# Mixture layers: the first turn's weight units before TensorE's branch, and buffers freed by ScalarE

## The reference

```python
g_sel = argmax(p_g); w_g = max(p_g)              # top-1 of 4 groups
top_v, top_i = lax.top_k(sel, 2)                 # top-2 of the 8 experts in the group
gate = w_g[:, None] * softmax(top_v)
y = (silu(x @ w_gate[e]) * (x @ w_up[e])) @ w_down[e]   # 32 experts, width 256
out[token] += y * gate
```

## Time and profile before

| | us |
|---|---|
| runs before, median of 3 | 2005.03 (2000.83 to 2006.79) |
| the profiled execution | 2006.36 |
| its span, first to last instruction | 2004.5 |
| TensorE busy | 1783.8 (89%) |
| VectorE busy | 1085.9 (54%) |
| ScalarE busy | 644.9 (32%) |
| first mixture layer, from the router to its last addition | about 34 to 273.7 |
| second mixture layer | about 436 to 676.0 |

### The profile page before, as it was taken

The page is one execution under the profiler, slowest core; times in us unless marked ns, Lnnn a source line. Parts: engine busy times, 40 slices in busy tenths (PEclk is TensorE's granted clock), DMA queues, the critical chain, the costliest instruction groups (busy, mean ns, idle before and its releaser), DMA issues. The chain is left out here.

```text
span 2004.5 us, 29934 instructions
## 1 busy us (share of the span) xinstructions
PE 1783.8 (89%) x12646; PEld 1318.7 (66%) x12646; DVE 1085.9 (54%) x1973; ACT 644.9 (32%) x1013; POOL 10.5 (1%) x6
## 2 busy tenths in 40 slices
PE   6888789888887899989996999999998988769998
PEld 5332266573322588878875788878886877557887
DVE  4332243353322577742378586677666564558665
ACT  3111012241110444422233554455443502136443
POOL 0000000000000000000000000000000000100000
PEclk9898889788988899999997899999999989679999
DMA  9899971358999955513420355535542412044540
GB/s 362 368 420 421 421 280 36 132 196 360 422 420 421 384 181 184 182 59 114 181 84 1 126 210 187 188 129 195 187 167 95 147 41 87 4 147 168 189 168 22
DMA packets 58189, 405.26 MB, mean 202 GB/s; under 512 B 6416, under 2 KB 7824, under 8 KB 10432
## 3 DMA queue, kind: packets, MB, share of 16 engines
q1 hardware_dynamic: 58048, 403.25, 52.4%
HBM read 402.18 MB, written 1.05 MB: 201 GB/s over the span
## 5 line engine op out<-in xcount | busy, mean ns | idle before, releaser
L1995 PE MATMUL ps<-ffn_x,ffn_wh 128*128 128x512 f32 x1408 | 497.1, 407 | 9.9 <-DVE ffn_x L2129 7.1
L1998 PE MATMUL ps<-ffn_x,ffn_wl 128*128 128x256 f32 x1408 | 376.7, 281 | 0.0
L1995 PEld LDWEIGHTS ps<-ffn_x,ffn_wh 128*128 128x128 f32 x1408 | 270.1, 192 | 84.2 <-issue 11.0
L2136 DVE TENSOR_TENSOR ffn_wl<-w,ffn_wh 128x2048 fp32r<-128x2048 f32 x132 | 301.6, 2287 | 1.6
L1998 PEld LDWEIGHTS ps<-ffn_x,ffn_wl 128*128 128x128 f32 x1408 | 258.2, 189 | 1.6
L2080 ACT CAST ffn_wh<-w 128x2048 fp32r<-128x2048 f32 (+1 forms) x140 | 252.7, 1805 | 6.3 <-PEq L711 5.2
L2095 ACT COPY ffn_part_low<-ps 128x512 f32<-128x512 f32 x88 | 51.5, 586 | 339.0 <-PE ps L1998 338.7
L2140 DVE TENSOR_TENSOR ffn_z<-ps,ffn_part_low 128x512 f32<-128x512 f32 x88 | 60.8, 691 | 161.5 <-ACT ffn_part_low L2095 161.3
L2039 PE MATMUL ps<-ffn_wh,ffn_hidh 128*128 128x512 f32 x352 | 138.3, 393 | 0.4 <-issue 0.4
L2041 PE MATMUL ps<-ffn_wh,ffn_hidl 128*128 128x512 f32 x352 | 137.5, 391 | 0.0
L2040 PE MATMUL ps<-ffn_wl,ffn_hidh 128*128 128x512 f32 x352 | 137.3, 390 | 0.0
(11 more groups left out here) (537 smaller groups left out, 2709.1 us busy)
## 6 DMA issues: line engine op xcount, KB each, us to landing
w<-in_ffn_gu SPq DMA_DIRECT2D x88, 1024.0 KB, 4.8
w<-in_moe_gu SPq DMA_DIRECT2D x70, 1024.0 KB, 22.9
w_extra<-in_moe_gu SPq DMA_DIRECT2D x52, 1024.0 KB, 26.5
w<-in_ffn_dn SPq DMA_DIRECT2D x44, 1024.0 KB, 4.8
w_extra<-in_moe_dn SPq DMA_DIRECT2D x32, 1024.0 KB, 26.3
w<-in_moe_dn SPq DMA_DIRECT2D x26, 1024.0 KB, 26.8
sq<-in_moe_dn SPq DMA_DIRECT2D x6, 1024.0 KB, 28.0
sq<-in_moe_gu SPq DMA_DIRECT2D x6, 1024.0 KB, 27.9
```

The source lines that it names most:

```text
L1995: return nc.tensor.matmul(pair_of(b)[:, a], high[:, s, tile(a, k)], X[:, k], start=k == 0, stop=False)
L1998: return nc.tensor.matmul(pair_of(b)[:, a, 0:SEQ], low[:, s, tile(a, k)], XH[:, k], start=False, stop=k == KT - 1)
L2136: nc.vector.tensor_tensor(low[:, s], S.buf(units[n]), high[:, s], ALU.subtract).then_inc(*w_split.one())
```

## The change

- TensorE, ahead of its branch: besides turn 0's gather and transposes, all eight gate and up units of turn 0 and both halves of `gather(1)`, interleaved. The second half of `gather(0)` is split so that `turn_x(0, 0)` comes after its first two matmuls.
- These eight units raise a new semaphore, `gu_ahead`, and not `gu_done`. ScalarE waits for each, does a copy of one column into `of_quad`, and that raises `gu_done`.
- ScalarE does nothing ahead of its branch any more. In its arm it first frees the eight units, with `take_slots(1, 0)` between.
- VectorE takes over turn 0's four copies, and `choose(1)` comes ahead of the branch; copies and `choose(1)` stand ahead of the gate computation, the last copy behind it.
- Behind the branch TensorE begins with `turn_x(1)`; `turn_gates(0)` moves behind the first unit of turn 1.
- In the last turn, `by_token(7)` for channel groups 0 to 3 comes ahead of the last down unit, and VectorE's second `split_y` moves behind the fourth addition.

```diff
@@ -755,7 +755,6 @@
             routing["scalar"](act)
             act.wait_ge(*counted.at(1))
             fullest = K.fullest(act, count)
-            in_slots["scalar_first"](act)
             with act.If(fullest > CAP):
                 over_all["scalar"](act)
...
-        build_first(dve, 0)
+        choose_first(dve, 0)
         dve.wait_ge(*x_taken.at(2))
         low(1)
+        copy_first(dve)
+        choose_first(dve, 1)
+        copy_second(dve)
...
         dve.wait_ge(*priced.now())
+        copy_last(dve)
...
+        def gather(i, half, parts=(0, 1, 2)):
+
+            if 0 in parts:
+                if half == 0:
+                    pe.wait_ge(sel_made.sem, i + 1)
+                    if i >= 2:
+                        pe.wait_ge(hidT_made.sem, i - 1)
+                elif i >= 2:
+                    pe.wait_ge(spread_taken.sem, i - 1)
+                if i == 0:
+                    pe.wait_ge(*x_taken.at(half + 1))
+                    pe.wait_ge(*xl_made.at(half + 1))
+            f, to = slice(half * 512, (half + 1) * 512), K.ps[:, 2 + half, :]
+            for t in parts:
+                if t < 2:
+                    nc.tensor.matmul(to, sel[:, i % 2, t], xh[:, t, f], start=t == 0, stop=False)
+                    nc.tensor.matmul(to, sel[:, i % 2, t], xl[:, t, f], start=False, stop=False)
+                else:
+                    nc.tensor.matmul(to, selr[:, i % 2], xr[:, f], start=False, stop=True).then_inc(x_made.sem, 1)
...
-                pe.wait_ge(xs_a.sem, i + 2 if i else 1)
-            elif i:
-                pe.wait_ge(xs_v.sem, i)
+                pe.wait_ge(xs_v.sem, half + 1)
+            elif half == 0:
+                pe.wait_ge(xs_a.sem, i)
             else:
-                pe.wait_ge(xs_a.sem, 2)
+                pe.wait_ge(xs_v.sem, i + 2)
             for k in range(4):
                 mm = nc.tensor.transpose(K.ps[:, 2 + half, k * P:(k + 1) * P], xs[:, half, k * P:(k + 1) * P], K.con(C_ID))
             mm.then_inc(x_made.sem, 1)
...
-                mm.then_inc(gu_done.sem, 1)
+                if ahead:
+                    mm.then_inc(gu_ahead.sem, 1)
+                else:
+                    mm.then_inc(gu_done.sem, 1)
...
-        def down(i):
+        def down(i, halves=(0, 1), ks=range(ET)):
 
             pe.wait_ge(hidT_made.sem, i + 1)
-            for half in range(2):
+            for half in halves:
                 if i:
                     pe.wait_ge(y_split.sem, 2 * i - 1 + half)
-                for k in range(ET):
+                for k in ks:
                     u = dn[4 * i + 2 * half + k]
...
         if first:
             gather(0, 0)
-            gather(0, 1)
+            gather(0, 1, (0,))
             turn_x(0, 0)
+            gather(0, 1, (1, 2))
+            pe.wait_ge(xg_v.sem, 1)
+            gate_up(0, (0, 1), ahead=True)
             turn_x(0, 1)
+            gate_up(0, (2, 3), ahead=True)
+            gather(1, 0)
+            pe.wait_ge(xg_v.sem, 2)
+            gate_up(0, (4, 5), ahead=True)
+            gather(1, 1)
+            gate_up(0, (6, 7), ahead=True)
             return
-        pe.wait_ge(xg_a.sem, 1)
-        gate_up(0, (0, 1, 2, 3))
-        gather(1, 0)
-        gather(1, 1)
-        gate_up(0, (4,))
         turn_x(1, 0)
-        gate_up(0, (5,))
         turn_x(1, 1)
-        gate_up(0, (6,))
-        turn_gates(0)
-        gate_up(0, (7,))
+        pe.wait_ge(*gu_done.at(KT))
         for i in range(1, TURNS):
-            pe.wait_ge(xg_a.sem, i + 2)
-            gate_up(i, (0, 1))
-            turn_hidden(i - 1)
-            gate_up(i, (2, 3))
+            pe.wait_ge(xg_a.sem, i)
+            if i == 1:
+                gate_up(i, (0,))
+                turn_gates(0)
+                gate_up(i, (1, 2))
+                turn_hidden(0)
+                gate_up(i, (3,))
+            else:
+                gate_up(i, (0, 1))
+                turn_hidden(i - 1)
+                gate_up(i, (2, 3))
             down(i - 1)
             if i == TURNS - 1:
                 turn_gates(i)
                 by_token(i - 1, range(0, 4))
                 by_token(i - 1, range(4, KT))
-                pe.wait_ge(xg_v.sem, i)
+                pe.wait_ge(xg_v.sem, i + 2)
                 gate_up(i, (4, 5, 6, 7))
                 continue
             gather(i + 1, 0)
             gather(i + 1, 1)
-            pe.wait_ge(xg_v.sem, i)
+            pe.wait_ge(xg_v.sem, i + 2)
             gate_up(i, (4,))
             turn_x(i + 1, 0)
             gate_up(i, (5,))
@@ -1096,11 +1111,13 @@
             gate_up(i, (7,))
             by_token(i - 1, range(4, KT))
         turn_hidden(TURNS - 1)
-        down(TURNS - 1)
+        down(TURNS - 1, (0,))
+        down(TURNS - 1, (1,), range(ET - 1))
         by_token(TURNS - 1, range(0, 4))
+        down(TURNS - 1, (1,), range(ET - 1, ET))
         by_token(TURNS - 1, range(4, KT))
...
-        if first:
-            take_slots(0, 0)
-            take_slots(0, 1)
-            take_x(0, 0)
-            take_x(0, 1)
-            return
+        for k in range(KT):
+            if k == 4:
+                take_slots(1, 0)
+            act.wait_ge(gu_ahead.sem, k + 1)
+            if k >= 4:
+                act.wait_ge(*gu_done.at(k - 3))
+            nc.scalar.copy(of_quad[:, k % 4:k % 4 + 1], K.con(C_QUAD, 1)).then_inc(gu_done.sem, 1)
...
+            if i and i + 1 < TURNS:
+                take_slots(i + 1, 0)
             if i + 1 < TURNS:
-                take_slots(i + 1, 0)
                 take_x(i + 1, 0)
...
+        def take_slots(i, half=1):
+            dve.wait_ge(x_made.sem, 4 * i + 1 + half if i else 2 * half + 1)
+            v.tensor_copy(xs[:, half], K.ps[:, 2 + half]).then_inc(xs_v.sem, 1)
+
+        def take_x(i, half=1):
+            dve.wait_ge(x_made.sem, 4 * i + 3 + half if i else 2 * half + 2)
+            v.tensor_copy(xg[:, i % 2, 4 * half:4 * half + 4], K.ps[:, 2 + half].rearrange("p (k s) -> p k s", k=4)).then_inc(xg_v.sem, 1)
...
         for i in range(TURNS + 1):
             if i:
...
-            if i + 1 < TURNS:
+            if i and i + 1 < TURNS:
                 choose(i + 1)
             if i:
                 split_y(i - 1, 0)
+            if i and i < TURNS:
                 split_y(i - 1, 1)
             if i + 1 < TURNS:
                 take_slots(i + 1)
                 take_x(i + 1)
             if i:
                 for m in range(KT):
+                    if i == TURNS and m == 4:
+                        split_y(i - 1, 1)
                     dve.wait_ge(back.sem, KT * (i - 1) + m + 1)
                     v.tensor_tensor(K.h[:, m], K.h[:, m], K.ps[:, 6 + m % 2, 0:L1], ALU.add).then_inc(added.sem, 1)
```

More of the change, by code:

```diff
@@ L765, in _ @@
         def _(dve):
-            routing["vector"](dve, in_slots["vector_first"])
+            routing["vector"](dve, in_slots["choose_first"], in_slots["copy_first"], in_slots["copy_second"], in_slots["copy_last"])
             dve.wait_ge(*counted.at(1))
@@ L869, in scalar, with vector @@
         nc.scalar.activation(small[:, :, 57:58], small[:, :, 56:57], ACT.Exp).then_inc(*exd.one())
-    def vector(dve, build_first):
+    def vector(dve, choose_first, copy_first, copy_second, copy_last):
         def do(ins):
@@ L964, in experts_in_slots @@
     s = lambda name: Signal(nc, f"slot_{name}_{layer}")
-    sel_made, gate_ready, x_made, xs_a, xs_v, xg_a, xg_v = (s(n) for n in ("sel", "gated", "x_made", "xs_a", "xs_v", "xg_a", "xg_v"))
+    sel_made, gate_ready, x_made, xs_a, xs_v, xg_a, xg_v, gu_ahead = (s(n) for n in ("sel", "gated", "x_made", "xs_a", "xs_v", "xg_a", "xg_v", "gu_ahead"))
     spread_made, spread_taken = s("spread"), s("spread_out")
@@ L971, in tensor, with turn_x @@
     def tensor(pe, first=False):
-        def gather(i, half):
-            if half == 0:
-                pe.wait_ge(sel_made.sem, i + 1)
-                if i >= 2:
-                    pe.wait_ge(hidT_made.sem, i - 1)
-            elif i >= 2:
-                pe.wait_ge(spread_taken.sem, i - 1)
-            elif i == 1:
-                pe.wait_ge(xg_a.sem, 2)
-            if i == 0:
-                pe.wait_ge(*x_taken.at(half + 1))
-                pe.wait_ge(*xl_made.at(half + 1))
-            f, to = slice(half * 512, (half + 1) * 512), K.ps[:, 2 + half, :]
-            for t in range(2):
-                nc.tensor.matmul(to, sel[:, i % 2, t], xh[:, t, f], start=t == 0, stop=False)
-                nc.tensor.matmul(to, sel[:, i % 2, t], xl[:, t, f], start=False, stop=False)
-            nc.tensor.matmul(to, selr[:, i % 2], xr[:, f], start=False, stop=True).then_inc(x_made.sem, 1)
-        def turn_x(i, half):
-            if half == 0:
-                pe.wait_ge(xs_a.sem, i + 2 if i else 1)
-            elif i:
-                pe.wait_ge(xs_v.sem, i)
+        def gather(i, half, parts=(0, 1, 2)):
[16 more added lines that the diff above has]
```

(38 more changed lines are left out.)

8 lines of the change are left out of this document (1 added, 7 removed).

## The result

| | before | changed |
|---|---|---|
| median of 10 runs each, same chip, us | 2005.91 (1999.56 to 2014.31) | 1994.97 (1985.52 to 2000.94) |
| ratio, 95% interval | | 0.995 (0.9937 to 0.9962) |
| profiled execution, us | 2006.36 | 1995.17 |
| its span, us | 2004.5 | 1993.3 |

1994 was forecast and 1994.97 measured, inside the range. The kernel is 0.5% faster: the medians differ by 10.9 us here, and by 8.2 us when both kernels ran again on another chip (first experiment).

The account below looks back on a forecast made before the run. The weight stream was taken to bound the mixture layers; 10.1 us from their starts plus 1.0 from their ends, 11.1, off the profiled 2006.36 gave 1995.3, median 1993.9, stated as 1994; range 1987 to 2002.

Parts of the forecast that it names:

- What bounds it: Both mixture layers: the weight stream bounds them, standing still once at each start, for 5.7 and 5.9 us.
- Loses that time for good: Mixture layers: where the weight stream stands still, 5.7 and 5.9 us at the starts, the layer never regains that time.
- The first unit and the first issue: First layer's start: unit 0 starts at 56.3 instead of 62.19; first freed buffer's issue at 58.2, before 64.17.
- the term of 10.1 us: Start of both layers: an earlier first freed buffer shortens the stream's standstill, gaining 5.5 and 4.6 us.
- ScalarE's branch: Turn 0: a code fetch of 3.3 to 7.05 us, covered by TensorE's unit 0, so cost nothing.
- the rival of a second fetch: At the new branches: a second instruction fetch gives part of the gain back; gain 5, time 2000; chance 0.13.
- TensorE's branch under a full stream: Behind unit 7 of turn 0: the branch costs 5.0 us, up to 7.05; unit 8 freed at 75.4.
- The margin: At TensorE's branch: unit 8 freed at 75.4, issue needed by 78.2; 2.8 us spare, 0.7 at 7.05.
- TensorE catches up: After its branch, TensorE, 3 us further behind the stream, recovers within two or three turns; nothing is paid.
- The slower rival: At both branches: a fetch waits for the whole DMA queue; 8.6 us worse, less 1.0, time 2012.6; chance 0.06.
- The end of the layer: Last turn: four channel groups fill the wait for the last unit; gain 0.5 a layer, bounds -0.5 and 1.2.
- The sum: Whole kernel: 10.1 from the starts plus 1.0 from the layer ends, 11.1 us gained; gain 8 to 14 had chance 0.74.

Follow-up runs that it names:

- first experiment: The changed kernel again, no edit, against the kernel before on another chip: median 1994.02 us, ratio 0.9955.
- ScalarE's wait: Changed kernel, but ScalarE waits ahead of its branch until the fourth weight unit is done: median 1998.09 us, ratio 0.9979 to the kernel before.
- four units ahead: Changed kernel with only the first four weight units ahead of TensorE's branch instead of eight: median 1998.86 us, ratio 0.9982 to the kernel before.
- the repeat: The changed kernel run again without edit, against the kernel before on another chip: median 1994.02 us, ratio 0.9955.
- a fill cut to the waits: Not tried: fewer idle matmuls in TensorE's two routing waits; changed kernel with 12 and 6 of them: 1994.86 us, ratio 0.9959 to before.

## Why the prediction was right

*What bounds it: shown.* Without the standstill the last unit lands 4.2 and 4.4 us earlier; putting 4.1 and 3.4 us of standstill back with ScalarE's wait makes it 3.2 and 3.4 later; a second standstill, four units ahead, costs as well. "Loses that time for good" was a little too strong, next point.

*The first unit and the first issue: right.* 56.3 forecast and 56.52 measured; 58.2 and 57.88. The start came 0.2 us later than forecast and the issue 0.3 earlier, because the unit was shorter than the 1.4 us that I took for a clock that rises within it. Stretch of the changed kernel:

```profile
57.00:58.00 1.00, 1.00 (x16) 0.24 (x8) 0.90 (x5) 0.19 (x1) 0.00 (x0) 1.00 1.02 426
```

The clock was back at full at about 56.4 (0.90 in 56 to 58, 1.00 in 57 to 58), so unit 0 ran at full clock: two units in 1.92 us. That is this execution; in the repeat and in the second layer the half clock reached into the unit. The standstill shrank by 5.6 and 5.2 us, forecast 5.5 and 4.6. But of this the last unit's landing shows 4.2 and 4.4, so the term of 10.1 us measured 8.6. In the repeat it measured 7.7 (3.1 and 4.6), with the standstill shorter by 4.1 and 5.2. Summed over all DMA engines the bytes of that unit had moved 5.7 and 4.7 us earlier than before; the trace has sixteen semaphore updates for each issue, and the landing is the last of them; it came behind that moment by a lag that grew from 1.5 and 1.9 to 3.0 and 2.2 (repeat 3.1 and 2.1). Why is open; it grew by under 2 us in both layers.

*ScalarE's branch: cost right (nothing), reason wrong.* I covered a fetch of 3.3 to 7.05 us with TensorE's unit 0. With nothing to cover it, wait, branch and release took 0.5 and 0.25 us. Its early place is not needed. That also lets the rival of a second fetch fall on ScalarE; on TensorE the idle time was 4.04 and 4.10, no sign of one (other kernels' layers had up to 5.11, about the 5.0 that I took).

*TensorE's branch under a full stream: right.* 5.0 forecast, 4.04 idle measured. I had unit 8 freed at 75.4, and the next issue stands at 75.62. The two errors that cancel: unit 7 ended at 67.7 and the branch cost 1 us less, but behind the branch TensorE ran at half clock (0.50 in 70 to 82), so transposes and unit 8 took 3.8 us instead of 2.2. The margin, 2.8 us, held. That TensorE catches up was right too: full clock and 44.70 of 50 us busy in 110 to 160.

*The slower rival, a fetch behind the whole queue: refuted.* DMA queues of the changed kernel in 69 to 70 us, while TensorE stands at its branch:

```profile
q1 hardware_dynamic: 57, 0.37, 92.0%
q8 instruction: 1, 0.02, 6.8%
q14 instruction: 1, 0.01, 2.0%
```

Instruction packets move here, 1.3 to 2.3 us after unit 7 has ended, and some 2 us later TensorE goes on. For which engine they are the view does not say; that TensorE goes on at 71.72 is what decides. By then 24 units had been issued (16, then 8 until 67.97) and some 20 moved (16 by 59.3, one per 2.5 us since), so the whole queue would have lasted until about 79, some 7 us past the moment at which TensorE went on. The rule of the Trainium skill that the prediction weighed (DMA: Bandwidth & Descriptors, section on queues, rings and completion order: each engine goes round its queues by the packet) agrees with this.

*The end of the layer: forecast 0.5 and 0.5, measured -0.4 and 1.3.* The size of the sum was right, the step that I worked out was not. I had TensorE at the last unit 1.1 us late, always. At full clock it is 0.5 late and gains 1.0. With half clock on the last units, one takes 1.94 instead of 1.06 us and the four groups 2.4 (262.40 to 264.83) instead of 1.8: 1.9 late, and the gain is gone. The old order waits for the last unit instead, so half clock ahead of it would cost it less; no profile of the old order has half clock in the last 8 us before the landing, so that is not shown. I put the first layer's end at 267.7; it came at 269.71, 1.3 us by the stream's term and 0.9 by this one, less 0.2 for an earlier start.

*The sum.* 8.6 for 10.1 from the stream, 0.9 for 1.0 from the ends, 1.8 for nothing from the unchanged rest: 11.2 for 11.1. Two misses cancelled: the stream gave less than forecast, and the unchanged rest came out 1.8 us shorter, which is inside the scatter. The mechanism was right; that the total agrees so closely is luck. With the repeat's layers averaged in, the layers give 223.2 + 223.1 - 220.0 - 217.4 = 8.9.

What stays open: why the half clock falls where it does in the last turn, why the landing gains less than the standstill loses, and what a fill cut to the waits would bring.

## What to carry to other kernels

Where a weight stream bounds, look in the stretches for the places at which it stands still, and ask which buffer comes free first and what stands between its reader and that moment; most of the time taken away there reaches the end (here 8.6 of 10.8 us, 7.7 of 9.3 in the repeat). A branch that costs a fetch belongs where enough buffers have just been freed: count units freed ahead of it times the time of one against the idle time behind it. At the end of such a stream, filling the last wait with work gains only as long as the work is shorter than the wait at the slower clock too.

## What the hardware showed that was not expected

- The same branch cost TensorE 4.0 to 5.1 us (4.04, 4.10, 4.21 and 5.11 in the rows above) and ScalarE, with its wait and release, 0.5 and 0.25 us. ScalarE showed no wait for its code although its other arm is long too; why wasn't tested.
- A branch under a full stream cost TensorE about as much (4.04 and 4.10; 4.21 and 5.11 with four units ahead) as beside an empty one (4.72, 3.28).
- TensorE's granted clock stood at half in 48 to 56, in 70 to 82 (behind the gap of the branch) and most of 257 to 265 us of the changed kernel, and in the last turns it fell on different units in different executions. From landing to end the same new end took 5.3 to 7.3 us.
- An fp32 matmul of 128 x 272 takes 0.47 us (5.67 / 12) at full clock, as two recorded ones.
